# One opening stage in place of two, and a conditioning round moved into the layer norm, in a one-core transformer kernel on Trainium2

## The chip, the cores and the metric

The kernel runs on one core of a Trainium2 chip. The metric is the device time of one execution in microseconds (us); lower is better. All computation is in float32. A weight matrix and its input are each split into a high part that TensorE multiplies in a rounded format (fp32r) and a low remainder, and a product is made of three of the four partial products.

## What is computed

The reference is a chain of transformer blocks. The change touches only the first of them, the convolution block of layer 0, on 512 latent and 256 context tokens of width 1024:

```python
sc = silu(c); scc = silu(c_ctx)
mod_lat = sc @ ada_w[i] + ada_b[i]          # i = 0, 1; six vectors of 1024 each
mod_ctx = scc @ ada_w[i] + ada_b[i]
sh1, sc1, g1, sh2, sc2, g2 = split(mod_lat, 6)      # and the same for ctx
a = rmsnorm(h, norm1_g[i]) * (1 + sc1) + sh1
u = a @ w_pw1 + b_pw1
a, g = split(u, 2)
v = dwconv(a * sigmoid(g), w_dw, 31 taps) + b_dw
v = silu(layernorm(v, ln_g, ln_b))
h = h + g1 * (v @ w_pw2 + b_pw2)
```

The rest (feed-forward blocks, window attention, latent attention, memory attention and a mixture of 16 experts) stands in both kernels as it is.

## The kernel before, in words

Activations lie with the 1024 features on 128 partitions in 8 chunks (KD = 8) and the 768 tokens along the free axis. `X` is the residual, `XNH` and `XNL` the high and low part of the input of the next product. The work is a list of stages. Each stage is a block with a program of its own for every engine, and ends in a barrier of all engines. SP (SyncE) issues every load here, on one DMA queue, in the order of its program.

**Conditioning.** The product of the two conditioning vectors with `ada_w` (2 x 1024 x 6144) is cut into rounds of 8 slices, each slice 1 MB (128 partitions x 4 x 512 numbers). The class `Ada` runs rounds `first` to `end`. Its slices go through a ring of four buffers `ADAW`: `load` (L383) fetches slice n, `multiply_slice` (L405) waits for it and makes four products of 512 columns and counts the semaphore `used`, and SP may load slice n + 4 when slice n is used. After the eighth slice ScalarE copies the result into `ADAR` (`keep_round`, L422), TensorE turns it onto the partitions (`turn_round`, L414), and VectorE adds the bias and makes `MOD`, `GAIN` and `G1B` (`finish`, L431 to L441). Round 0 yields shift and scale of the first norm, rounds 1 and 2 the gate and the other vectors of layer 0, round 3 the shift and scale of layer 1's first norm, which no stage needs before the feed-forward stage of layer 0 is over.

**Stage `start`** loads three small tensors (`PRM`, `IDENT`, `DELTA`) and makes the silu of the conditioning vectors (`SC`).

**Stage `ada`** (`condition`) runs round 0. SP loads its eight slices, then the residual `X` (3 MB), then the first four weight units `RAW` of `pw1` (0.5 MB each). ScalarE and VectorE then split units 0 and 1 into `WHI` (L472) and `WLO` (L480).

**Stage `pw1`** (`gated_convolution`) begins with the class `Norm`: ScalarE squares the 8 chunks of `X` (L546), TensorE sums them over the partitions (L506), ScalarE takes the root (L549), VectorE inverts it (L572), TensorE spreads it over the partitions (L514). Then the 8 chunks pass through VectorE (`SQ`, L579), ScalarE (`SCALED` L556, which needs `MOD` and `GAIN`, and `XNH` L560) and VectorE (`XNL` L582), and `multiply_first` (L329) multiplies units 0 and 1 chunk by chunk as these come. The other 14 units follow (L278). Beside them VectorE convolves chunks 0 to 3 with 31 taps each (L592, L595). Chunks 4 to 7 of the convolution are made on TensorE (`convolve`, L758) at the end of the stage, out of copies of `V` shifted by 8 tokens (`V4`, 16 small copies per chunk, `shift_chunk`, L635). ScalarE moves each result back (`keep_chunk`, L677). Rounds 1, 2 and 3 of the conditioning stand between and behind them on TensorE:

```python
            convolve(0)
            for i in range(ada.rounds):
                convolve(i + 1)
                ada.multiply_round(pe, i)
```

**Stage `pw2`** (`project`) begins with `LayerNormSilu`: TensorE sums for the mean (L506), VectorE centres (L831), ScalarE squares (L798), TensorE sums (L506), ScalarE takes the root into `NARROW` (L802), VectorE inverts it (L834), TensorE spreads it (L514), and the chunks pass VectorE (L841), ScalarE (L808, L811) and VectorE (L845). `multiply_first` takes units 0 and 1, and units 2 to 7 follow. Each unit's result is scaled on ScalarE (L882) and added to `X` on VectorE (L900). The split of unit 2's weights (L249, L260) waits for the end of unit 0.

## Time and profile before

| what | value |
|---|---|
| median of 3 runs | 2690.73 us (2686.09 to 2698.99) |
| profiled execution | 2687.36 us, its span 2685.5 us |
| TensorE (PE) busy | 2437.6 us, 91% of the span |
| VectorE (DVE) busy | 1207.5 us, 45% |
| ScalarE (ACT) busy | 841.2 us, 31% |
| HBM read | 380.22 MB, 142 GB/s over the span |

The profiled execution took 1.9 us more than its span. The busy share is an average over all stages. The change acts only on the first 420 us or so, and there the question is at each place which engine or transfer the others wait for. So the rows below are of the timeline (instructions in order of time, with the idle time before them and what ended it) and of windows (busy time of each engine, granted TensorE clock and DMA share in a stretch).

### The profile page before, as it was taken

What the parts mean: (1) busy time and instruction counts of PE and PEld (TensorE: products, weight loads), DVE (VectorE), ACT (ScalarE), POOL (GpSimd) and SP (SyncE); (2) the same over time, 40 slices, a digit from 0 to 9 for tenths busy, and PEclk for the clock granted to TensorE, in tenths of its full rate; (3) what the DMA queues carried; (4) which work ended last, traced back from release to release, by engine and by line L of the source; (5) the groups of instructions that cost most, each with busy time, mean ns of one, the idle gap of its engine ahead of it and who ended that gap; (6) DMA issues with size and microseconds to landing.
All of it is one profiled execution on the core that took longest, in us unless ns stands there. A gap on an engine that the chain in (4) does not pass through costs nothing. (4 is left out here: it accounts for less than half of the span.)

```text
span 2685.5 us, 34858 instructions
## 1 busy us (share of the span) xinstructions
PE 2437.6 (91%) x14152; PEld 1744.2 (65%) x14152; DVE 1207.5 (45%) x1785; ACT 841.2 (31%) x1290; POOL 29.7 (1%) x57
## 2 busy tenths in 40 slices
PE   4988798999999989899899999987997889999987
PEld 2873376888888876567688888865885653333322
DVE  2598144553255323375465465654543332222223
ACT  3210145332133223276443244355434321000001
POOL 0000000000000000100000000000000000000000
PEclk7998798999999999899899999999999889999998
DMA  5137511121112222400223232210340359999996
GB/s 228 56 89 254 203 48 40 63 72 62 56 62 69 73 102 113 172 1 25 80 100 110 79 105 98 78 53 5 114 133 21 144 198 411 408 411 411 411 414 244
DMA packets 93555, 390.85 MB, mean 146 GB/s; under 512 B 9072, under 2 KB 33904, under 8 KB 65264
## 3 DMA queue, kind: packets, MB, share of 16 engines
q1 hardware_dynamic: 93424, 388.97, 38.9%
q8 instruction: 98, 1.61, 0.2%
q14 instruction: 33, 0.27, 0.0%
HBM read 380.22 MB, written 2.10 MB: 142 GB/s over the span
## 5 line engine op out<-in xcount | busy, mean ns | idle before, releaser
L278 PE MATMUL PS<-XNH,WHI 128*128 128x512 f32 (+1 forms) x1888 | 593.0, 358 | 26.0 <-DVE WLO L260 10.1
L260 DVE TENSOR_TENSOR WLO<-RAW,WHI 128x1024 fp32r<-128x1024 f32 (+3 forms) x226 | 279.2, 1236 | 722.6 <-ACT WHI L249 722.5
L278 PE MATMUL PS<-XNH,WLO 128*128 128x512 f32 (+1 forms) x1888 | 587.9, 355 | 0.0
L278 PE MATMUL PS<-XNL,WHI 128*128 128x512 f32 (+1 forms) x1888 | 587.3, 355 | 0.0
L249 ACT ACTIVATE WHI<-RAW 128x1024 fp32r<-128x1024 f32 (+3 forms) x226 | 241.5, 1068 | 890.5 <-PE PS L278 870.5
L278 PEld LDWEIGHTS PS<-XNH,WHI 128*128 128x128 f32 x1888 | 320.6, 189 | 86.6 <-issue 19.9
L278 PEld LDWEIGHTS PS<-XNL,WHI 128*128 128x128 f32 x1888 | 320.5, 189 | 52.6 <-issue 1.0
L278 PEld LDWEIGHTS PS<-XNH,WLO 128*128 128x128 f32 x1888 | 320.0, 189 | 51.8
L2565 PE MATMUL PS<-RAWM,XS 128*64 128x512 f32 x912 | 216.5, 602 | 19.0 <-DMA RAWM<-experts 18.3
L278 PE MATMUL PS<-HH,WHI 128*128 128x512 f32 (+1 forms) x528 | 158.4, 354 | 0.1
L278 PE MATMUL PS<-HH,WLO 128*128 128x512 f32 (+1 forms) x528 | 158.2, 354 | 0.0
L278 PE MATMUL PS<-HL,WHI 128*128 128x512 f32 (+1 forms) x528 | 158.2, 354 | 0.0
L2565 PEld LDWEIGHTS PS<-RAWM,XS 128*64 128x64 f32 x912 | 59.0, 136 | 143.3 <-issue 76.3
L595 DVE SCALAR_TENSOR_TENSOR C<-V,PRM,C (+1 forms) x120 | 126.0, 1050 | 11.8 <-DVE C L595 9.4
L2699 DVE TENSOR_TENSOR X<-PS,X 128x1024 f32<-128x1024 f32 x64 | 76.8, 1222 | 99.6 <-PE PS L2598 99.6
L2565 PE MATMUL PS<-RAWM,HT 128*64 128x512 f32 x456 | 106.7, 601 | 0.0
L278 PEld LDWEIGHTS PS<-HH,WHI 128*128 128x128 f32 x528 | 86.4, 188 | 15.4 <-DVE HL L1015 0.9
L278 PEld LDWEIGHTS PS<-HH,WLO 128*128 128x128 f32 x528 | 86.4, 188 | 14.6
L278 PEld LDWEIGHTS PS<-HL,WHI 128*128 128x128 f32 x528 | 86.4, 188 | 14.5
L405 PE MATMUL PS<-ADAW,SC 128*32 128x512 f32 x384 | 61.9, 755 | 32.8 <-DMA ADAW<-ada 32.8
L1007 DVE SCALAR_TENSOR_TENSOR Y<-PS,PRM,Y 128x511 f32<-128x511 f32 (+1 forms) x132 | 83.2, 658 | 10.6 <-DVE Y L1002 9.7
L2731 DVE TENSOR_TENSOR HT<-PS,SIL 128x512 f32<-128x512 f32 x16 | 11.1, 692 | 165.5 <-PE PS L2585 165.5
(346 smaller groups left out, 2681.7 us busy)
## 6 DMA issues: line engine op xcount, KB each, us to landing
RAWM<-experts SPq DMA_DIRECT2D x171, 1024.0 KB, 16.2
ADAW<-ada SPq DMA_DIRECT2D x48, 1024.0 KB, 8.3
RAW<-up SPq DMA_DIRECT2D x88, 512.0 KB, 3.2
RAW<-down SPq DMA_DIRECT2D x32, 704.0 KB, 4.1
X<-experts SPq DMA_DIRECT2D x21, 1024.0 KB, 18.4
RAW<-pw SPq DMA_DIRECT2D x24, 512.0 KB, 3.4
V<-V SPq DMA_DIRECT2D x64, 101.0 KB, 2.6
RAW<-qkv SPq DMA_DIRECT2D x12, 512.0 KB, 3.3
```

The source lines that it names most:

```text
L249: act.activation(prog.WHI[:, at % SPLITS, 0:to.length], prog.RAW[:, at % RAWS, 0:to.length], ACT.Copy).then_inc(prog.weights_hi, 1)
L260: dve.tensor_tensor(prog.WLO[:, at % SPLITS, 0:to.length], prog.RAW[:, at % RAWS, 0:to.length], f32(prog.WHI[:, at % SPLITS, 0:to.length]) ...
L278: last = pe.matmul(prog.PS[:, to, a:b], w, x[:, k, a:b], start=(k == 0 and n == 0), stop=(k == g.k - 1 and n == 2))
L405: last = pe.matmul(self.products[n // KD][32 * j:32 * j + 32, :], self.prog.SC[:, k, :], self.ring[:, n % ADA_RING, j * 512:(j + 1) * 512] ...
L595: steps.did(dve.scalar_tensor_tensor(out, v, w, out, ALU.mult, ALU.add))
L1007: ins = dve.scalar_tensor_tensor(Y[:, s, a:b - 1], prog.PS[:, slot, a + 1:b], coef(grp, i, s, 2), Y[:, s, a:b - 1], ALU.mult, ALU.add)
L2565: last = pe.matmul(ps[64 * half:64 * half + 64, :], x(k), moe.half[slot](2 * n + half), start=(k == 0), stop=(k == KD - 1))
L2699: dve.tensor_tensor(x, PAIRS_PS[pair], x, ALU.add).then_inc(added, 1)
L2731: dve.tensor_tensor(HT[:].rearrange("p c h s -> p (c h s)"), BT_PS, SIL[:].rearrange("p c h s -> p (c h s)"), ALU.mult).then_inc(hidden, 1)
```

## The change

The stage `ada` is gone. Its parts stand in `start` and `pw1`:

- In `start`, SP issues, behind the three small loads, the residual in two halves of four chunks, and the first four slices of round 0.
- In `pw1`, SP issues `RAW` units 0 and 1, then slices 4 to 7 as buffers come free, then units 2 and 3.
- TensorE makes the sums of the norm, slices 0 to 3, the spread, slices 4 to 7, and the turn. ScalarE makes squares and root, the split of units 0 and 1, `ADAR`, and only then the chunks. VectorE makes the first two chunks of `SQ`, then `WLO` and `finish`, then the rest.
- In the tail of `pw1`, only rounds 1 and 2 are left. The order is convolve 0, convolve 1, round 1, convolve 2, convolve 3, round 2. The copies for chunk 3 are issued ahead of slice 8 and not of slice 10. Behind the last slice, SP issues the first three slices of round 3 into three buffers of their own (`ADAL`).
- `pw2` is a function of its own, `convolution_output`. Its TensorE multiplies slices 0 and 1 of round 3 ahead of the spread, 2 and 3 behind it, and 4 to 7 behind units 0 and 1, waits until ScalarE has kept the round (their sum lies in the bank that unit 2 writes), and turns it between units 6 and 7. SP loads slice n (3 to 7) when slice n - 3 is used, and all of that ahead of its weight loads.

```diff
+def load_first_slices(prog, sp):
+    prog.first_ring = prog.at("ADAW_0", [P, ADA_RING, 4 * 512], F32, prog.arena + 45536)
+    for n in range(2):
+        sp.dma_start(prog.X[:, 4 * n:4 * n + 4, :], prog.dram["xT"][:, 4 * n:4 * n + 4, :]).then_inc(prog.x_landed[n], 16)
+    for n in range(ADA_RING):
+        sp.dma_start(prog.first_ring[:, n, :], prog.dram["ada"][n]).then_inc(prog.ada_first[n], 16)
...
-def condition(prog, first):
...
+            for u in range(RAWS):
+                if u == SPLITS:
+                    first.load_rest(sp)
+                sp.dma_start(prog.RAW[:, u, 0:g.length], g.src[u]).then_inc(prog.raw_landed[u], 16)
...
             for n in range(ADA_RING, KD * ada.rounds):
-                if n == KD + 2:
+                if n == KD:
                     shift_chunk(3)
                 sp.wait_ge(ada.used, n - ADA_RING + 1)
                 ada.load(sp, n)
+            sp.wait_ge(convolved, 3)
+            for n, slot in enumerate(late_ring):
+                sp.dma_start(slot, prog.dram["ada"][3 * KD + n]).then_inc(prog.ada_landed[n], 16)
...
         def _(act):
-            before.on_scalar(act)
+            before.statistics_on_scalar(act, lambda k: act.wait_ge(prog.x_landed[k // 4], 16))
+            for u in range(SPLITS):
+                act.wait_ge(prog.raw_landed[u], 16)
+                act.activation(prog.WHI[:, u, 0:g.length], prog.RAW[:, u, 0:g.length], ACT.Copy).then_inc(prog.weights_hi, 1)
+            first.keep_round(act, 0)
+            act.wait_ge(first.step, 2)
+            before.chunks_on_scalar(act)
...
-            before.on_tensor(pe)
+            before.sums_on_tensor(pe)
+            for n in range(ADA_RING):
+                first.multiply_slice(pe, n)
+            before.spread_on_tensor(pe)
+            for n in range(ADA_RING, KD):
+                first.multiply_slice(pe, n)
+            first.turn_round(pe, 0)
...
             convolve(0)
-            for i in range(ada.rounds):
-                convolve(i + 1)
-                ada.multiply_round(pe, i)
+            convolve(1)
+            ada.multiply_round(pe, 0)
+            convolve(2)
+            convolve(3)
+            ada.multiply_round(pe, 1)
...
+def convolution_output(prog, g, gate, bias):
...
+        def _(sp):
+            for n in range(3, KD):
+                sp.wait_ge(ada.used, n - 2)
+                ada.load(sp, n)
+            for u in range(g.n):
+                load_ahead(prog, sp, g, u // 4, u % 4)
...
+                ins.then_inc(scaled, 1)
+                if u == 0:
+                    ada.keep_round(act, 0)
...
+            norm.on_tensor(pe)
+            pe.nop().then_inc(psum_free, 4)
+            multiply_first(prog, pe, g, prog.XNH, prog.XNL, lambda u: BOTH, psum_free, chunks_of(pe, norm))
+            for n in range(4, KD):
+                ada.multiply_slice(pe, n)
+            pe.wait_ge(ada.kept, 1)
+            for u in range(2, g.n):
+                multiply(prog, pe, g, u // 4, u % 4, prog.XNH, prog.XNL, BOTH, psum_free)
+                if u == 6:
+                    pe.wait_ge(psum_free, 4 + 5)
+                    ada.turn_round(pe, 0)
```

SP, from the program's start to the first weight loads of `pw1`'s loop (`xT` is the residual in memory, `ada` the conditioning weights, `pw` the weights of `pw1` and `pw2`). Before:

```order
L345 DMA DELTA<-delta 128x32
L173 UNCONDITIONAL_BRANCH
L452 UNCONDITIONAL_BRANCH
L383 DMA ADAW_127<-ada 128x2048 x8
L456 DMA X<-xT 128x6144
L458 DMA RAW<-pw 128x1024 x4
```

Now:

```order
L357 DMA DELTA<-delta 128x32
L344 DMA X<-xT 128x3072 x2
L346 DMA ADAW_101<-ada 128x2048 x4
L175 UNCONDITIONAL_BRANCH
L625 UNCONDITIONAL_BRANCH
L640 DMA RAW<-pw 128x1024 x2
L402 DMA ADAW_101<-ada 128x2048 x4
L640 DMA RAW<-pw 128x1024 x2
```

The residual moved from behind all eight slices to ahead of them, across the first barrier, and two weight units moved ahead of slices 4 to 7.

SP, from the last weight unit of `pw1`'s own loads to the loads of the feed-forward stage (`V` is the shifted copy). Before:

```order
L238 DMA RAW<-pw 128x1024
L383 DMA ADAW_244<-ada 128x2048 x4
L635 DMA V_2_239<-V_235 32x808 x16
L383 DMA ADAW_244<-ada 128x2048 x6
L635 DMA V_2_239<-V_235 32x808 x16
L383 DMA ADAW_244<-ada 128x2048 x14
L173 UNCONDITIONAL_BRANCH
L862 UNCONDITIONAL_BRANCH
L238 DMA RAW<-pw 128x1024 x4
```

Now:

```order
L402 DMA ADAW_146<-ada 128x2048 x4
L634 DMA V_1_141<-V_137 32x808 x16
L402 DMA ADAW_146<-ada 128x2048 x8
L662 DMA ADAL_147<-ada 128x2048
L662 DMA ADAL_148<-ada 128x2048
L662 DMA ADAL_149<-ada 128x2048
L175 UNCONDITIONAL_BRANCH
L899 UNCONDITIONAL_BRANCH
L402 DMA ADAL_147<-ada 128x2048
L402 DMA ADAL_148<-ada 128x2048
L402 DMA ADAL_149<-ada 128x2048
```

Of the 24 slices of the tail 16 are left in it, 3 are issued at its end, and 5 stand in `pw2` ahead of its weight loads.

TensorE in `pw2`, around its spread (L494) and around unit 2 (L280; units 0 and 1 are L331):

```order
L486 MATMUL PS<-TMP_2458,ONES 32x64 x4
L424 MATMUL PS<-ADAL_147,SC 32x512 x4
L424 MATMUL PS<-ADAL_148,SC 32x512 x4
L494 MATMUL PS<-NARROW_2460,IDENT 128x128 x4
L494 MATMUL PS<-NARROW_2460,IDENT 128x64 x4
L424 MATMUL PS<-ADAL_149,SC 32x512 x4
L424 MATMUL PS<-ADAL_147,SC 32x512 x4
L331 MATMUL PS<-XNH,WHI 128x512
...
L331 MATMUL PS<-XNH,WLO 128x256
L424 MATMUL PS<-ADAL_148,SC 32x512 x4
L424 MATMUL PS<-ADAL_149,SC 32x512 x4
L424 MATMUL PS<-ADAL_147,SC 32x512 x4
L424 MATMUL PS<-ADAL_148,SC 32x512 x4
L280 MATMUL PS<-XNH,WHI 128x512
```

None of the L424 rows stood here before. There the spread followed the sums, and unit 2 followed units 0 and 1.

## Rows read from the trace of the kernel before

**Rows 1.** Windows: the opening, and a stretch of pw1's tail (columns in the first line).
```profile
core 0: us, PE busy (x) PEld busy (x) DVE busy (x) ACT busy (x) POOL busy (x), PEclk, DMA share, GB/s
0.00:40.00 40.00, 15.11 (x72) 3.31 (x72) 3.24 (x7) 4.58 (x6) 0.20 (x4) 0.75 0.88 356
...
240.00:260.00 20.00, 15.00 (x112) 4.48 (x116) 19.33 (x20) 0.60 (x1) 0.00 (x0) 0.74 1.01 354
```
**Rows 2.** Timeline of the opening: start, duration, engine, line, operation, idle before.
```profile
4.50 0.22 ACT L351 ACTIVATE SC<-PRM 128x16 f32<-128x16 f32 x1 [1.85 <-DMA DELTA<-delta]
4.98 14.58 SPq L383 DMA_DIRECT2D ADAW<-ada  x8
...
9.83 1.94 PE L405 MATMUL PS<-ADAW,SC 128*32 128x512 f32 x8 [9.83 <-DMA ADAW<-ada]
...
27.18 1.94 PE L405 MATMUL PS<-ADAW,SC 128*32 128x512 f32 x8 [1.43 <-DMA ADAW<-ada]
...
31.97 0.18 DVE L437 SCALAR_TENSOR_TENSOR GAIN<-MOD,PRM 128x16 f32<-128x16 f32 x1
35.74 1.06 ACT L472 ACTIVATE WHI<-RAW 128x1024 fp32r<-128x1024 f32 x1 [5.96 <-DMA RAW<-pw]
...
39.63 1.58 ACT L546 ACTIVATE SQ<-X 128x768 f32<-128x768 f32 x2 [1.56 <-PEq L173]
...
53.28 1.30 ACT L556 ACTIVATE SCALED<-SQ,MOD,GAIN 128x512 f32<-128x512 f32 x2 [5.03 <-DVE SQ L579]
...
56.60 0.98 PE L329 MATMUL PS<-XNH,WHI 128*128 128x512 f32 x2 [4.34 <-DVE XNL L582]
```
**Rows 3.** Timeline of TensorE in pw1's tail.
```profile
236.09 3.61 PE L405 MATMUL PS<-ADAW,SC 128*32 128x512 f32 x32
242.48 1.93 PE L405 MATMUL PS<-ADAW,SC 128*32 128x512 f32 x8 [2.78 <-DMA ADAW<-ada]
...
252.98 11.88 PE L758 MATMUL PS<-V,DIAG 128*32 128x512 f32 x128
264.69 1.89 PE L405 MATMUL PS<-ADAW,SC 128*32 128x512 f32 x16
...
284.92 10.54 PE L758 MATMUL PS<-V,DIAG 128*32 128x512 f32 x128
295.27 3.62 PE L405 MATMUL PS<-ADAW,SC 128*32 128x512 f32 x32
```
**Rows 4.** Timeline: ScalarE and VectorE at the end of pw1.
```profile
310.86 0.60 ACT L422 ACTIVATE ADAR<-PS 128x512 f32<-128x512 f32 x1 [14.29 <-PE PS L405]
...
312.61 0.32 DVE L431 TENSOR_TENSOR MOD<-PS,PRM 128x64 f32<-128x64 f32 x2 [41.82 <-PE PS L414]
```
**Rows 5.** Timeline of SP's queue in pw1's tail (start, length of issuing).
```profile
237.35 9.92 SPq L383 DMA_DIRECT2D ADAW<-ada  x6
247.38 11.94 SPq L635 DMA_DIRECT2D V<-V  x16
```
**Rows 6.** Timeline of pw2: the inversion, the spread, units 0 and 1, unit 2.
```profile
331.54 1.35 DVE L834 RECIPROCAL NARROW<-NARROW 128x192 f32<-128x192 f32 x1 [3.14 <-ACT NARROW L802]
332.95 3.67 PE L514 MATMUL PS<-NARROW,IDENT 128*128 128x128 f32 x16 [2.41 <-DVE NARROW L834]
...
340.75 0.98 PE L329 MATMUL PS<-XNH,WHI 128*128 128x512 f32 x2 [4.13 <-DVE XNL L845]
...
361.05 0.62 PE L278 MATMUL PS<-XNH,WHI 128*128 128x512 f32 x2 [1.41 <-DVE WLO L260]
```
**Rows 7.** Windows on the granted clock (PEclk) after waits: pw1's tail, pw2, pw1's start.
```profile
299.00:309.00 10.00, 4.94 (x24) 0.56 (x24) 0.00 (x0) 0.00 (x0) 0.00 (x0) 0.73 0.93 378
...
340.70:345.00 4.30, 4.25 (x15) 3.66 (x16) 4.12 (x8) 4.07 (x5) 0.00 (x0) 0.56 0.00 0
345.00:359.60 14.60, 14.60 (x84) 12.45 (x82) 7.80 (x13) 8.49 (x10) 0.00 (x0) 1.00 0.00 1
...
56.60:61.00 4.40, 4.40 (x14) 3.72 (x14) 3.90 (x5) 4.30 (x8) 0.00 (x0) 0.50 0.02 4
```

More of the change, by code:

```diff
@@ L362, with ring_of, __init__ @@
 ADA_ROUNDS = 2 * ADA_SLICES // 4
+def ring_of(tile):
+    return [tile[:, s, :] for s in range(ADA_RING)]
 class Ada:
-    def __init__(self, prog, first, end, ring, rows, products=None, turned_at=None, sem=None):
+    def __init__(self, prog, first, end, ring, rows, products=None, turned_at=None, sem=None, landed=None):
         self.prog, self.first, self.rounds = prog, first, end - first
-        self.ring, self.rows = ring, rows
+        self.slots, self.rows = ring, rows
+        self.n_slots = len(ring)
         self.products = [prog.PS[:, 0, 0:512]] * self.rounds if products is None else products
@@ L376, in __init__ @@
         sem = sem or prog.sem
-        self.landed = [sem(f"ada_landed{s}") for s in range(ADA_RING)]
+        self.landed = [sem(f"ada_landed{s}") for s in range(self.n_slots)] if landed is None else landed
         self.used, self.kept, self.turned = sem("ada_used"), sem("ada_kept"), sem("ada_turned")
@@ L381, in load @@
     def load(self, sp, n):
-        sp.dma_start(self.ring[:, n % ADA_RING, :], self.src[KD * self.first + n]).then_inc(self.landed[n % ADA_RING], 16)
+        sp.dma_start(self.slots[n % self.n_slots], self.src[KD * self.first + n]).then_inc(self.landed[n % self.n_slots], 16)
     def load_first(self, sp):
-        for n in range(ADA_RING):
+        for n in range(self.n_slots):
             self.load(sp, n)
     def load_rest(self, sp):
-        for n in range(ADA_RING, KD * self.rounds):
-            sp.wait_ge(self.used, n - ADA_RING + 1)
+        for n in range(self.n_slots, KD * self.rounds):
+            sp.wait_ge(self.used, n - self.n_slots + 1)
             self.load(sp, n)
```

122 lines of the change are left out of this document (75 added, 47 removed).

## The prediction

> **What bounds the kernel now.** I read the windows first, to see which resource is full in the stretches that the change touches, and then the timeline of each place. In the opening 40 us the DMA queues are full (share 0.88, 356 GB/s) while TensorE is busy for 15.11 us [rows 1]. In the tail of `pw1` the same holds: DMA share 1.01 between 240 and 260 us with TensorE waiting for slices [rows 1, 3]. So both places wait for bytes or for a chain behind them, and an engine's busy share tells little.
>
> The opening is three chains in series [rows 2]. The slices come from 9.83 us on, and the eighth at 27.18, so one takes (27.18 - 9.83) / 7 = 2.48 us, or 423 GB/s. `GAIN` is ready at 31.97 + 0.18 = 32.15. Then come `X` and the weights (35.74) and a barrier, and only at 39.63 do the squares begin. Statistics last until ScalarE's first scaled chunk at 53.28, and the first product stands at 56.60. The statistics need only `X`. `GAIN` is first needed at 53.28, 21 us after it is ready.
>
> The tail is a chain of TensorE and slices. VectorE ends its taps 41.82 us before `MOD` [rows 4], so it doesn't bound the end. A round takes TensorE 3.61 us for four slices that lie in the ring, and then follows DMA: the last one goes from 295.27 to 310.86, 15.59 us [rows 3, 4].
>
> **The opening.** The small loads have landed at 4.50 [rows 2]. Now `X` and the first slices are issued behind them with no barrier between, so bytes flow on from about 4.5. Ahead of the last slice's landing stand `X` (3.15 MB), eight slices (8.39 MB) and two units (1.05 MB), 12.58 MB, at 423 GB/s 29.7 us: it lands at 34.2, against 27.18 before. Can SP keep the queue full? `X` has landed at about 12. The last four squares take 4 x 0.79 = 3.2 us, so sums end near 16, and slices 0 to 3 at the lower clock take 1.94 each [rows 2]: the last is used near 24. Slices 4 to 7 are therefore issued between 18 and 24, while the queue holds work until 24.2 (12 for `X`, four slices to 21.9, two units to 24.4). It just suffices. Root, inversion and spread, which took 53.28 - 39.63 = 13.7 us with the squares before, now end near 28, under the remaining slices. The split of the two units hides there too. From the last slice to `GAIN` it was 32.15 - 27.18 = 4.97 us, so `GAIN` is at 39.2, and from ScalarE's first scaling to the first product it was 56.60 - 53.28 = 3.32: first product at 42.5. That is **-14.1 us**. Lower bound of the gain: if slice 0 is used late and the last four slices come as slowly as they come when SP waits for one buffer each, two to three more intervals of 2.48 are lost, gain 7. Upper bound: 15.
>
> After that `pw1` has the same work in the same order and shifts as a whole.
>
> **The tail of `pw1`.** I keep the old times here. Up to 252.98 nothing changes: convolve 0 and 1 and one round. Convolve 2 runs to 264.69 [rows 3]. Now convolve 3 follows at once; it took 295.27 - 284.92 = 10.35 us in one place and 11.71 in the other, which began at the lower clock. I take 10.35, since it now stands right behind a dense stretch: 275.0. Then the last round, whose first four slices must lie in the ring. SP issues the copies right behind slice 7 (near 240) for 11.9 us [rows 5], then slices 8 to 11, which land from about 257 to 269 even if the copies hold the queue for as long as they are issued; cover 6 us. So the round lasts 15.59 as before and `ADAR` is kept at 290.6 and not at 310.86: **-20.2 us**. If convolve 3 takes 11.71, -18.9. If the cover fails altogether (four slices still to come at 275), +10 on that, -10. The three late slices are issued behind all others and land by 298, over 10 us ahead of their first use.
>
> **The norm of `pw2`.** Slices 0 and 1 stand in TensorE's wait ahead of 332.95, which is 2.41 us long [rows 6]. At 1.94 each they last 3.9, at the rate of 3.61 for four 1.8. So the spread is late by at most 1.5 us. But the spread took 3.67 there at the lower clock, and denser work ahead of it may shorten it. Slice 3 is issued when slice 0 is used (about 332) and lands about 5 us later (issued at 237.35, multiplied at 242.48 [rows 3, 5]), 337.5; slices 2 and 3 end by 339.5, ahead of the first chunk at 340.75. TensorE then comes to units 0 and 1 from work and not from a wait of 4.13 us. These ran from 340.75 to 359.65 (361.05 - 1.41), 18.9 us, with the granted clock at 0.56 in the first 4.3 us (most of it the lower level, 1.2 GHz) and at 1.00 behind [rows 7]. With the full clock from the start, 0.44 x 4.3 = 1.9 less. I take **-1.9**, between +1.5 (all slices slow, no clock won) and -3.5.
>
> **Slices 4 to 7 of `pw2`.** This is the new wait. Slices 4, 5 and 6 lie in the three buffers, but slice 7 takes slice 4's buffer and is issued only when that is used. The pattern is that of a round: from its first slice to the fifth's arrival 242.48 - 236.09 = 6.39 us [rows 3]. So slice 7 starts at 359.65 + 6.4 = 366.0. Then 0.9 to 1.9 for it (over a round's slices that come by DMA the granted clock is 0.73 [rows 7], so either is possible), and 0.7 for ScalarE's copy (310.86 + 0.60, and a semaphore): unit 2 begins at 367.7 to 368.6 and not at 361.05, +6.7 to +7.6. Behind unit 2's start ScalarE has been waiting too, with the split of unit 3 behind it, and SP with the weight loads; both are needed a whole unit later, so they cost nothing. TensorE has waited some 3.7 us and more. After waits of 4.13 and 4.34 us it had 0.56 and 0.50 of the clock for the next 4.3 [rows 2, 6, 7], which costs half of that, +1.9. I take **+9.0**, between +6.5 and +10.
>
> The Trainium skill, TensorE: Matmul & The Clock Gate, section The HAM clock gate, says that the throttled state is the default, that activity releases it, and that work arriving in bursts behind DMA waits pays the lower clock again each time. By that, the gain of a warm start and the loss behind the new wait both stand (-1.9 and +1.9), and the change is no free filling of waits. Those two sizes are taken from the rows, and the trace agrees.
>
> **The turn** between units 6 and 7 stands in a dense stretch: from `ADAR`'s copy at 310.86 to `MOD` at 312.61 it is 1.75, less the copy's 0.60 [rows 4], **+1.2**.
>
> For slice 7 the row gives about 5.1 us from issue to use. The Trainium skill, DMA: Bandwidth & Descriptors, section Anatomy of one DMA, gives a fixed cost of about 2.0 us and a peak of 436 GB/s. An estimate from these, 2.0 + 1.05 MB / 436 GB/s = 4.4, would make the wait 0.7 shorter and the sum -26.7; I go by the row.
>
> **Sum:** -14.1 - 20.2 - 1.9 + 9.0 + 1.2 = **-26.0 us**. The profiled execution, 2687.36, becomes 2661.4. The median of the runs shown is 3.4 above it and theirs spread over 13 us, so I state the median: 2690.73 - 26.0 = **2664.7**. The rest of the program comes behind one barrier and shifts.
>
> **The rivals.**
>
> 1. *One of the two places gives half.* Either SP finds the ring full in the opening (gain 7), or the copies delay slices 8 to 11 (gain 10). For it: in the opening the queue and the use of the buffers meet within about 1 us. Against: the tail has a cover of 6 us. Sum -16 to -19, a time of 2672 to 2675. Chance 0.12.
> 2. *`pw2` eats most.* Round 3 is fetched there one buffer at a time. If each of slices 3, 4 and 7 has TensorE waiting a full 5.1 us, with the clock lost behind each (1.9), two more such waits cost 14. Sum -12, a time of 2679. For it: the ring is of three and not four. Against: slices 4 to 6 have the 19 us of units 0 and 1 to land. Chance 0.07.
> 3. *Slower than before, by the clock.* `pw1`'s 16 units now start out of a thin stretch of slices. If the clock stayed at its lower level there, each unit would take 8.5 us more (a unit is 18.9 - 1.9 = 17.0 for two). It turns the result slower from four such units on (34 against 26); at six it is 2716. Against: the clock came back within 4.4 us of the first product in the same place, after an equally thin opening [rows 7]. Chance 0.03.
> 4. *More than forecast*, where the tail's convolve and the norm take the better ends and slice 7 comes early: -31, 2660. This lies inside my forecast's own spread.
>
> **How the numbers follow.** My forecast holds 0.78. The likeliest case's terms give -20 to -33 (2658 to 2671), and a median of few runs moves by some 4 us. Taking in rival 1 the range is 2653 to 2676, which leaves out rivals 2 and 3 and a little on the low side. What a measurement can tell from no change is 0.5%, 13.5 us: faster means below 2677.3. All of the forecast and of rival 1 lie below, and a part of rival 2 by the noise: faster 0.90, same 0.07, slower 0.03.
>
> **What would show it.** The first L331 product at 42.5 us, 14 us sooner, with slices arriving without a gap; the last `ADAR` of `pw1` some 34 us sooner than 310.86, with copies and slices 8 to 11 landed before convolve 3 ends; no idle time ahead of the first chunk of `pw2` longer than 2 us and a PEclk near 1.00 in its first 4 us; between unit 1 and unit 2 about 8 us, with one DMA wait in it of some 3.7 us ahead of the fourth slice, and a lower clock behind. I am wrong if VectorE or the queue ends one of these waits instead, if the slices' spacing in the opening grows beyond 2.5 us, or if unit 2 doesn't wait.

## The result, and the profile after

| | before | changed |
|---|---|---|
| median, 8 runs each | 2698.76 us | 2664.97 us |
| lowest and highest | 2686.09, 2704.20 | 2661.64, 2680.35 |
| span of the profiled execution | 2685.5 us | 2663.0 us |

The ratio of changed to before is 0.990, with a 95% interval of 0.9883 to 0.9918: some 27 us less, between 22 and 32. Forecast were 26.0 us less and 2664.7 us. The two medians lie 33.8 us apart, which is more than the interval allows: runs of one kernel spread over 18 to 19 us, and the medians alone are less steady than the ratio over all runs. That the median fell within 0.3 us of the forecast is luck. The forecast was counted down from 2690.73, the median of three runs, and the median of eight is 8 us higher.

A table of marks shows where the time went. Each mark is the start of a row of the timeline, for the profiled execution of either kernel. A second profiled execution of the changed kernel (run `e10_changed_again` below) stands beside it.

| mark | before | changed | change of the stretch, changed against before | changed again |
|---|---|---|---|---|
| first product of `pw1` | 56.60 | 44.66 | -11.9 | 43.45 |
| first product of convolve 0 | 212.71 | 200.51 | -0.3 | 199.12 |
| last `ADAR` of `pw1` | 310.86 | 280.21 | -18.5 | 279.97 |
| first product of `pw2` | 340.75 | 308.29 | -1.8 | 308.08 |
| unit 2 of `pw2` | 361.05 | 335.49 | +6.9 | 333.67 |
| first square of the feed-forward stage | 415.77 | 393.07 | +2.9 | 390.80 |
| end of the span | 2685.5 | 2663.0 | +0.2 | 2672.5 |

**The opening.** Timeline of the changed kernel (start, duration, engine, line, operation, idle before), to be held against [rows 2]:

```profile
2.14 0.91 SPq L344 DMA_DIRECT2D X<-xT  x2
3.09 2.51 SPq L346 DMA_DIRECT2D ADAW<-ada  x4
...
9.83 1.58 ACT L531 ACTIVATE SQ<-X 128x768 f32<-128x768 f32 x2 [4.36 <-DMA X<-xT]
...
19.03 6.28 SPq L402 DMA_DIRECT2D ADAW<-ada  x4
...
26.89 1.82 DVE L572 TENSOR_TENSOR SQ<-X,PS 128x768 f32<-128x768 f32 x2 [6.53 <-PE PS L494]
...
28.89 1.06 PE L424 MATMUL PS<-ADAW,SC 128*32 128x512 f32 x8 [2.03 <-DMA ADAW<-ada]
...
36.35 1.94 PE L424 MATMUL PS<-ADAW,SC 128*32 128x512 f32 x8 [0.55 <-DMA ADAW<-ada]
...
41.35 1.30 ACT L543 ACTIVATE SCALED<-SQ,MOD,GAIN 128x512 f32<-128x512 f32 x2 [2.40 <-DVE GAIN L456]
...
44.66 0.98 PE L331 MATMUL PS<-XNH,WHI 128*128 128x512 f32 x2 [3.79 <-DVE XNL L577]
```

The statistics are over at 26.89, under the slices, and what ScalarE's first scaling waits for is now `GAIN`. The four last slices arrive 2.48 us apart (28.89 to 36.35), so the queue never ran empty. The last one came 2.1 us later than I had put it (34.2).

**The tail.** TensorE's timeline, to be held against [rows 3]:

```profile
223.79 3.60 PE L424 MATMUL PS<-ADAW,SC 128*32 128x512 f32 x32
229.95 1.94 PE L424 MATMUL PS<-ADAW,SC 128*32 128x512 f32 x8 [2.56 <-DMA ADAW<-ada]
232.43 1.94 PE L424 MATMUL PS<-ADAW,SC 128*32 128x512 f32 x8 [0.55 <-DMA ADAW<-ada]
234.92 1.84 PE L424 MATMUL PS<-ADAW,SC 128*32 128x512 f32 x8 [0.55 <-DMA ADAW<-ada]
239.40 1.47 PE L424 MATMUL PS<-ADAW,SC 128*32 128x512 f32 x8 [2.65 <-DMA ADAW<-ada]
241.57 1.87 PE L433 MATMUL PS<-PRM,ADAR 128*128 128x8 f32 x8 [0.70 <-ACT ADAR L441]
243.37 22.51 PE L787 MATMUL PS<-V,DIAG 128*32 128x512 f32 x256
265.71 3.60 PE L424 MATMUL PS<-ADAW,SC 128*32 128x512 f32 x32
```

Convolve 2 and 3 follow each other (22.3 us for both), and the next round begins with four slices in the ring. But in the first round slice 7 is late: it comes 4.48 us behind slice 6, not 2.48. The last `ADAR` of `pw1` stands 30.7 us sooner than before (280.21 against 310.86), where I had said some 34.

**The stage `pw2`.** Timeline around the norm, to be held against [rows 6]:

```profile
299.31 2.92 PE L424 MATMUL PS<-ADAL,SC 128*32 128x512 f32 x16
...
302.16 2.00 PE L494 MATMUL PS<-NARROW,IDENT 128*128 128x128 f32 x16
304.09 1.07 PE L424 MATMUL PS<-ADAL,SC 128*32 128x512 f32 x8
...
306.11 1.06 PE L424 MATMUL PS<-ADAL,SC 128*32 128x512 f32 x8 [0.95 <-DMA ADAL<-ada]
...
308.29 0.98 PE L331 MATMUL PS<-XNH,WHI 128*128 128x512 f32 x2 [1.11 <-DVE XNL L884]
```

Slices 0 and 1 fill the wait ahead of the spread, and the spread takes 2.00 us and not 3.67. Around unit 2:

```profile
326.91 2.78 PE L424 MATMUL PS<-ADAL,SC 128*32 128x512 f32 x24
...
332.83 1.94 PE L424 MATMUL PS<-ADAL,SC 128*32 128x512 f32 x8 [3.14 <-DMA ADAL<-ada]
334.83 0.60 ACT L441 ACTIVATE ADAR<-PS 128x512 f32<-128x512 f32 x1 [6.63 <-PE PS L424]
...
335.49 1.01 PE L280 MATMUL PS<-XNH,WHI 128*128 128x512 f32 x2 [0.72 <-ACT ADAR L441]
```

Slices 4 to 6 are multiplied at once, slice 7 is waited for, and unit 2 starts 335.49 - 326.91 = 8.58 us behind unit 1's end, where it had been 1.41. The windows tell the clock (columns as in [rows 1]):

```profile
303.00:308.00 5.00, 3.22 (x27) 1.34 (x26) 2.76 (x5) 2.72 (x3) 0.00 (x0) 1.00 0.96 401
308.30:312.00 3.70, 3.70 (x13) 3.17 (x14) 3.52 (x7) 3.48 (x5) 0.00 (x0) 0.55 0.93 359
...
335.50:340.00 4.50, 4.50 (x17) 3.87 (x18) 2.09 (x2) 2.00 (x3) 0.00 (x0) 0.62 0.35 133
```

Behind the new wait the granted clock is 0.62 for 4.5 us, and at the first product of `pw2` it fell to 0.55 although it had been 1.00 under slices 2 and 3.

### The profile page after: what moved, and what is told of

It reads as the page before. It is cut to its first block and busy times, and to the rows that moved or that the text cites. A ratio compares the mean times of both kernels' runs of the same rounds, so it can differ in the third digit from the quotient of the medians.

```text
span 2663.0 us, 34851 instructions
## 1 busy us (share of the span) xinstructions
PE 2430.8 (91%) x14152; PEld 1742.9 (65%) x14152; DVE 1207.0 (45%) x1785; ACT 841.0 (32%) x1290; POOL 29.7 (1%) x57
## 5 line engine op out<-in xcount | busy, mean ns | idle before, releaser
L280 PE MATMUL PS<-XNH,WHI 128*128 128x512 f32 (+1 forms) x1888 | 593.8, 359 | 25.3 <-DVE WLO L262 8.9
L280 PE MATMUL PS<-XNL,WHI 128*128 128x512 f32 (+1 forms) x1888 | 587.0, 355 | 0.0
L280 PE MATMUL PS<-XNH,WLO 128*128 128x512 f32 (+1 forms) x1888 | 586.4, 355 | 0.0
L280 PEld LDWEIGHTS PS<-XNH,WHI 128*128 128x128 f32 x1888 | 320.6, 189 | 86.8 <-issue 19.5
L280 PEld LDWEIGHTS PS<-XNL,WHI 128*128 128x128 f32 x1888 | 321.2, 190 | 53.0 <-issue 1.0
L280 PEld LDWEIGHTS PS<-XNH,WLO 128*128 128x128 f32 x1888 | 319.8, 189 | 52.3
L280 PE MATMUL PS<-HH,WHI 128*128 128x512 f32 (+1 forms) x528 | 158.3, 354 | 0.0
L280 PE MATMUL PS<-HL,WHI 128*128 128x512 f32 (+1 forms) x528 | 158.1, 353 | 0.0
L280 PE MATMUL PS<-HH,WLO 128*128 128x512 f32 (+1 forms) x528 | 158.0, 353 | 0.0
L590 DVE SCALAR_TENSOR_TENSOR C<-V,PRM,C (+1 forms) x120 | 125.9, 1050 | 11.8 <-DVE C L590 9.4
L2797 DVE TENSOR_TENSOR X<-PS,X 128x1024 f32<-128x1024 f32 x64 | 76.8, 1221 | 100.6 <-PE PS L2696 100.6
L280 PEld LDWEIGHTS PS<-HH,WHI 128*128 128x128 f32 x528 | 86.4, 188 | 15.4 <-DVE HL L1113 0.9
L280 PEld LDWEIGHTS PS<-HL,WHI 128*128 128x128 f32 x528 | 86.4, 188 | 14.5
L280 PEld LDWEIGHTS PS<-HH,WLO 128*128 128x128 f32 x528 | 86.4, 188 | 14.4
L1105 DVE SCALAR_TENSOR_TENSOR Y<-PS,PRM,Y 128x511 f32<-128x511 f32 (+1 forms) x132 | 83.2, 658 | 10.6 <-DVE Y L1100 9.7
L1100 DVE SCALAR_TENSOR_TENSOR Y<-PS,PRM,Y 128x511 f32<-128x511 f32 (+1 forms) x132 | 82.6, 653 | 0.0
```

The costliest lines, as they stand in the source:

```text
L280: last = pe.matmul(prog.PS[:, to, a:b], w, x[:, k, a:b], start=(k == 0 and n == 0), stop=(k == g.k - 1 and n == 2))
L590: steps.did(dve.scalar_tensor_tensor(out, v, w, out, ALU.mult, ALU.add))
L1100: ins = dve.scalar_tensor_tensor(Y[:, s, a + 1:b], prog.PS[:, slot, a:b - 1], coef(grp, i, s, 0), Y[:, s, a + 1:b], ALU.mult, ALU.add)
L1105: ins = dve.scalar_tensor_tensor(Y[:, s, a:b - 1], prog.PS[:, slot, a + 1:b], coef(grp, i, s, 2), Y[:, s, a:b - 1], ALU.mult, ALU.add)
L2797: dve.tensor_tensor(x, PAIRS_PS[pair], x, ALU.add).then_inc(added, 1)
```

## The experiments

Each run is read at the marks above. Totals of single executions of one kernel differ by 10 us and more, and the last section shows where a large part of that arises. So a few microseconds are told from stretches, not from totals. The changed kernel was profiled twice: the "first" execution is that of the result above, the "second" that of `e10_changed_again`.

| run | median us (runs) | ratio to before, 95% interval |
|---|---|---|
| `e1_opening_only` | 2683.86 (10) | 0.9945, 0.9923 to 0.9968 |
| `e2_no_round3` | 2665.34 (4) | 0.9897, 0.9863 to 0.9931 |
| `e3_slices_inside` | 2669.65 (4) | 0.9908, 0.9875 to 0.9941 |
| `e4_copies_late` | 2665.31 (4) | 0.9897, 0.9860 to 0.9933 |
| `e5_units_behind_slices` | 2673.99 (2) | 0.9912, 0.9890 to 0.9935 |
| `e6_dense_norm` | 2666.21 (1) | |
| `e7_small_loads_behind` | 2673.92 (1) | |
| `e8_combined` | 2662.99 (4) | 0.9878, 0.9847 to 0.9909 |
| `e9_tail_only` | 2688.45 (6) | 0.9975, 0.9952 to 0.9997 |
| `e10_changed_again` | 2671.35 (6) | 0.9913, 0.9890 to 0.9937 |
| `e11_combined_again` | 2667.40 (6) | 0.9889, 0.9862 to 0.9916 |

### The two places apart

`e1_opening_only` has the new opening and before's tail and `pw2`:

```diff
-        ada = Ada(prog, 1, 3, ring_of(ring), rows)
+        ada = Ada(prog, 1, 4, ring_of(ring), rows)
...
-            convolve(0)
-            convolve(1)
-            ada.multiply_round(pe, 0)
-            convolve(2)
-            convolve(3)
-            ada.multiply_round(pe, 1)
+            convolve(0)
+            for i in range(ada.rounds):
+                convolve(i + 1)
+                ada.multiply_round(pe, i)
...
-    add("pw2", lambda: convolution_output(prog, gemms["pw2"], ...
+    add("pw2", lambda: project(prog, gemms["pw2"], ...
```

> The new opening with the tail of pw1 and the stage pw2 of the kernel before. Theory (the opening, the tail and pw2 add up independently): the first product of pw1 stands near 44.7 us as in the changed kernel (56.6 before), everything behind it is as before, so the span is 12 us shorter than before's, about 2673.5. Rival (a later part gives the opening's gain back, or the tail's gain needs the new opening): the span is under 8 us or over 16 us shorter, and the stretch from the first product to the last ADAR of pw1 is not the 254.3 us of before.

`e9_tail_only` is its complement, with before's stage `ada` and the new tail and `pw2`:

```diff
-            load_first_slices(prog, sp)
...
-            before.sums_on_tensor(pe)
-            for n in range(ADA_RING):
-                first.multiply_slice(pe, n)
-            before.spread_on_tensor(pe)
-            for n in range(ADA_RING, KD):
-                first.multiply_slice(pe, n)
-            first.turn_round(pe, 0)
+            before.on_tensor(pe)
...
+    add("ada", lambda: condition(prog, order[0]))
```

> The tail of pw1 and the stage pw2 of the changed kernel, with the opening of the kernel before (stage ada and all). Theory (the parts add): the first product stands at 56.6 us as before, the stretch from the convolution's first product to the last ADAR of pw1 is some 18.5 us shorter than before's 98.1, pw2 from there to the first square of the feed-forward stage is 8 us longer than before's 104.9, and that square comes 10.5 us sooner than 415.8, near 405. Rival (with the old opening the tail's gain is another, or the opening's 12 us weren't all its own): that square is under 6 or over 15 us sooner.

First product of `pw1` (first line) and first square of the feed-forward stage (second), timeline of `e1_opening_only`:

```profile
42.95 0.98 PE L331 MATMUL PS<-XNH,WHI 128*128 128x512 f32 x2 [3.79 <-DVE XNL L577]
...
404.30 6.74 ACT L531 ACTIVATE SQ<-X 128x768 f32<-128x768 f32 x8 [1.30 <-PEq L175]
```

The same of `e9_tail_only`:

```profile
56.62 0.98 PE L331 MATMUL PS<-XNH,WHI 128*128 128x512 f32 x2 [4.35 <-DVE XNL L615]
...
403.90 1.58 ACT L569 ACTIVATE SQ<-X 128x768 f32<-128x768 f32 x2 [1.62 <-PEq L175]
```

At the square, before stood at 415.77. The opening alone is 11.5 us ahead of that and the tail with `pw2` alone 11.9, together 23.3, where the changed kernel is 22.7 ahead in its first execution and 25.0 in its second. So the parts add, to within the 2.3 us between those two, and neither needs the other. Of the 13.65 us that `e1_opening_only` is ahead at its first product, 11.5 are left at the square; 1.6 of the loss lies between the last `ADAR` and the first product of `pw2` (31.5 us against 29.9 before), and half of that is the turn there, at the lower clock (1.88 us against 1.06). The stretch from the first product to the last `ADAR` was 254.7 us in `e1_opening_only` (254.3 before). In `e9_tail_only` the tail took 80.2 us (98.15 before), and from the last `ADAR` to the square it was 111.5 (104.9 before). The gain of the opening at its first product was 13.65 us in `e1_opening_only` and 11.9 and 13.15 in the two executions of the changed kernel. About half of this spread is the turn behind the last slice, which took 1.88 us at the lower clock in the first execution and 1.06 at the full one in the two others. The rest is the last slice itself, which took 1.94, 1.58 and 1.52 us, and its arrival (36.35, 36.30 and 35.86).

### What round 3 costs in its new place

`e2_no_round3` leaves the round out of `pw2`, with constants for what it would yield:

```diff
-            for n in range(4, KD):
-                ada.multiply_slice(pe, n)
-            pe.wait_ge(ada.kept, 1)
...
-                    step = ada.finish(dve, [(1, 0, 2)], [(1, 0)])
+                    dve.memset(prog.MOD[1][:, 0:16, :], 0.5)
+                    dve.memset(prog.GAIN[1][0][:], 1.0)
```

> The changed kernel with round 3 of the conditioning left out of pw2: its five late loads, eight slices, copy, turn and bias are gone, and layer 1's first norm gets constants for its shift and scale. It prices what round 3 costs in its new place. Theory: it costs the wait between units 1 and 2 (8.6 us against 1.4), half a clock behind it (1.6) and the turn (1.1), and it gives back 1.7 on the spread, which runs at the full clock only because slices stand ahead of it; so the span is 8 us shorter than the changed kernel's (about 2655) and the spread takes 3.7 us again in place of 2.0. Rival (the spread's gain has nothing to do with the slices): the spread stays at 2.0 us and the span is 10 us shorter.

Timeline of `e2_no_round3`, the spread, the first product and the first square:

```profile
304.12 3.67 PE L494 MATMUL PS<-NARROW,IDENT 128*128 128x128 f32 x16 [2.41 <-DVE NARROW L868]
...
311.93 0.98 PE L331 MATMUL PS<-XNH,WHI 128*128 128x512 f32 x2 [4.13 <-DVE XNL L879]
...
386.96 1.58 ACT L531 ACTIVATE SQ<-X 128x768 f32<-128x768 f32 x2 [1.35 <-PEq L175]
```

The spread is back at 3.67 us, so its 1.7 us are a gift of the slices ahead of it, as the theory had it. It took 3.68 in `e1_opening_only` too, and 2.00 in all ten executions that have the slices there. From the first product to the square it is 75.03 us here, 75.02 before, and 84.78 and 82.72 in the two executions of the changed kernel: the round costs 7.7 to 9.8 us there. It gives back 2.9 ahead of the first product (30.98 against 28.08). Net that is 4.8 to 6.9 us, where I had expected 8. But 0.8 of the 2.9 is the clock at `pw1`'s last turn, which both kernels have (1.88 us here, 1.06 there) and which no edit set. Without it the round costs 5.6 to 7.7. Out of `pw1` it took a whole round, for which the tail is 17.3 to 18.5 us shorter.

### What the wait between units 1 and 2 is

`e3_slices_inside` gives the loads the time of units 0 and 1:

```diff
-            multiply_first(prog, pe, g, prog.XNH, prog.XNL, lambda u: BOTH, psum_free, chunks_of(pe, norm))
-            for n in range(4, KD):
-                ada.multiply_slice(pe, n)
+            inside = {3: 4, 5: 5, 6: 6}
+            multiply_first(prog, pe, g, prog.XNH, prog.XNL, lambda u: BOTH, psum_free, chunks_of(pe, norm),
+                           between=lambda k: k in inside and ada.multiply_slice(pe, inside[k]))
+            ada.multiply_slice(pe, 7)
```

> The changed kernel with slices 4, 5 and 6 of round 3 multiplied inside units 0 and 1 (behind chunks 3, 5 and 6) and only slice 7 behind them. Nothing is left out. Theory (the wait between units 1 and 2 is the latency of slice 7, whose load waits for slice 4's buffer): slice 7 has landed, units 0 and 1 get 2.7 us longer, unit 2 begins about 1.7 us behind them and not 8.6 behind, at the full clock: 4.2 + 1.6 = about 6 us shorter than the changed kernel, span near 2657. Rival (the wait is the chain through ScalarE, which copies the round only behind unit 0's scaling): the wait stays over 4 us and the gain is under 2 us.

Timeline of `e3_slices_inside`, from the first product to unit 2:

```profile
310.97 0.58 PE L331 MATMUL PS<-XNH,WHI 128*128 128x512 f32 x2 [1.08 <-DVE XNL L886]
...
331.52 1.07 PE L426 MATMUL PS<-ADAL,SC 128*32 128x512 f32 x8
...
333.35 0.62 PE L280 MATMUL PS<-XNH,WHI 128*128 128x512 f32 x2 [0.76 <-ACT ADAR L443]
```

Slice 7 is there, and unit 2 begins 1.83 us behind units 0 and 1, at the full clock (0.62 us for the pair and not 1.01). From the first product to unit 2 it is 22.4 us and not 27.2, and from there to the square 56.2 and not 57.6: 6.2 us less. The rival, a chain through ScalarE, is out, since ScalarE's program was not touched. That 6.2 meets the 6 expected is partly luck, because here the first products of `pw2` ran at the full clock and in the first execution of the changed kernel at the lower one, which this edit doesn't set. Against the second execution (82.72 us from the first product to the square), in which they ran at the full clock too, the 78.60 are 4.1 less. The other executions at the full clock with slices 4 to 7 behind units 0 and 1 and nothing added to the norm took 82.2 to 83.2 (`e5`, `e7`, `e9`), the two others with the slices inside 78.8 and 78.7 (`e8`, `e11`). So the edit is worth about 4 us, and 4.2 of wait and 1.6 of clock had been expected.

### Why slice 7 was late in the tail

```diff
-                if n == KD:
+                if n == KD + 2:
                     shift_chunk(3)
```

> The changed kernel with the copies for chunk 3 issued ahead of slice 10, as before, and not ahead of slice 8. Theory (the copies move at half the bytes per second and share the queue with slices 5 to 7 that were issued just ahead of them): slice 7 of the tail's first round arrives 2.5 us behind slice 6 and not 4.5, so the step from round to convolve 2 is 16.9 us and not 19.6, and the copies still land before convolve 3: 2 to 2.7 us shorter than the changed kernel. Rival (the 2.7 us are chance of that execution or the clock): slice 7 is late again, or convolve 3 now waits for its copies, and the span doesn't change or grows.

Timeline of `e4_copies_late`, slices 4 and 7 of the tail's first round and the turn:

```profile
229.07 1.90 PE L424 MATMUL PS<-ADAW,SC 128*32 128x512 f32 x8 [2.38 <-DMA ADAW<-ada]
...
236.54 1.94 PE L424 MATMUL PS<-ADAW,SC 128*32 128x512 f32 x8 [1.43 <-DMA ADAW<-ada]
239.19 1.88 PE L433 MATMUL PS<-PRM,ADAR 128*128 128x8 f32 x8 [0.71 <-ACT ADAR L441]
```

From slice 4 to slice 7 it is 7.47 us, against 9.45 in the changed kernel, 9.12 and 9.20 in `e2_no_round3` and `e3_slices_inside`, which have the same order of copies. All thirteen executions part in the same way: 9.0 to 9.5 us in the eight with the early copies, 7.45 to 7.51 in the five with the late ones (before, `e1`, `e4`, `e8`, `e11`). So slice 7's lateness hangs on that order, though slice 7 is issued ahead of the copies either way. The step from the round to convolve 2 took 17.9 us and not 19.6 (16.9 was expected: the turn fell into the lower clock), and convolve 3 did not wait for its copies. The whole tail took 79.2 us against 79.7 to 81.3 in the eight with the early copies and an otherwise equal tail. In the two other tails of this kind with late copies, `e8_combined` and `e11_combined_again`, it took 77.3 and 76.8. There the turn and convolve 2 ran at the full clock, and convolve 3 began 1.3 and 1.7 us behind the end of convolve 2, as the rival had feared. The queue still moved the bytes at the copies' rate until about then (232 GB/s from 248 to 249 us in `e8_combined`, 380 in the next microsecond), so the copies are the likely cause of this gap. That is not shown, since the profile names nothing that ended it.

### What the opening is bound by

`e5_units_behind_slices` moves one megabyte from ahead of the last slice to behind it:

```diff
+            first.load_rest(sp)
             for u in range(RAWS):
-                if u == SPLITS:
-                    first.load_rest(sp)
                 sp.dma_start(prog.RAW[:, u, 0:g.length], g.src[u]).then_inc(prog.raw_landed[u], 16)
...
+            first.keep_round(act, 0)
             for u in range(SPLITS):
                 act.wait_ge(prog.raw_landed[u], 16)
...
-            first.keep_round(act, 0)
...
-                first.finish(dve, [(0, 0, 2)], [(0, 0)])
+                    if u == 0:
+                        first.finish(dve, [(0, 0, 2)], [(0, 0)])
```

> The changed kernel with weight units 0 and 1 of pw1 loaded behind slices 4 to 7 of round 0 and not ahead of them; ScalarE copies the round first and splits the units then, VectorE puts the bias between the two remainders. Theory (the opening is bound by the bytes ahead of the last slice): the last slice arrives two half-megabyte loads sooner, 33.9 and not 36.35 us; the units land at about 35.1 and 36.4, their splits end near 40, and the first product stands near 42.2 to 43 and not 44.7: 1.5 to 2.5 us sooner. Rival (the split is now the last thing, or SP can't issue the last slices sooner because TensorE uses the first ones late): the last slice arrives no more than 1 us sooner, or the first product is where it was or later, because it waits for WLO.

Timeline of `e5_units_behind_slices`, the last slice, the first scaling and the first product:

```profile
33.74 1.93 PE L424 MATMUL PS<-ADAW,SC 128*32 128x512 f32 x8 [1.44 <-DMA ADAW<-ada]
...
38.89 1.31 ACT L543 ACTIVATE SCALED<-SQ,MOD,GAIN 128x512 f32<-128x512 f32 x2 [0.66 <-DVE GAIN L456]
...
42.21 0.98 PE L331 MATMUL PS<-XNH,WHI 128*128 128x512 f32 x2 [3.94 <-DVE XNL L577]
```

The last slice comes 2.6 us sooner for 1.05 MB less ahead of it (2.5 us at 423 GB/s), and the first product 2.45 us sooner. The opening is bound by bytes ahead of the last slice. Without this edit the last slice came at 35.86 to 36.84 us in eight executions, so the 2.6 are clear of their scatter.

`e7_small_loads_behind` asks about the 2.1 us that I had missed:

```diff
-            sp.dma_start(prog.IDENT[:], prog.dram["ident"]).then_inc(loaded, 16)
-            sp.dma_start(prog.DELTA[:], prog.dram["delta"]).then_inc(loaded, 16)
             load_first_slices(prog, sp)
+            sp.dma_start(prog.IDENT[:], prog.dram["ident"]).then_inc(prog.small_landed, 16)
+            sp.dma_start(prog.DELTA[:], prog.dram["delta"]).then_inc(prog.small_landed, 16)
...
-            act.wait_ge(loaded, 48)
+            act.wait_ge(loaded, 16)
...
```

> The changed kernel with the two small loads IDENT and DELTA issued behind the residual and the first four slices, with waits of their own. I had put the last slice of round 0 at 34.2 us, and it came at 36.35. Theory (the two small loads, with rows of 512 and 128 bytes, slow the queues down while the residual starts): the first half of the residual lands at least 1 us sooner than 9.83 us and the last slice with it. Rival (the 2.1 us are the time from a transfer's last byte to its landing together with the queues' start, which order doesn't change): both stay within 0.5 us.

Timeline of `e7_small_loads_behind`, the first squares and the last slice:

```profile
8.41 1.58 ACT L532 ACTIVATE SQ<-X 128x768 f32<-128x768 f32 x2 [4.03 <-DMA X<-xT]
...
36.15 1.78 PE L425 MATMUL PS<-ADAW,SC 128*32 128x512 f32 x8 [0.56 <-DMA ADAW<-ada]
```

Half of each theory: the residual's first half lands 1.4 us sooner, the last slice 0.2. Of the 1.4 us, 0.9 is that SP issues the residual at 1.20 and not at 2.14. The 0.2 is within the scatter of the last slice, so it is no gain, and why the last slice doesn't follow the residual no run shows. With 12.58 MB at 423 GB/s ahead of it, a last slice at 36.35 means a stream that counts from 6.6 us, and I had let it count from 4.5, when the small loads had landed. Windows of the first execution allow an estimate of how these 2.1 us part. Up to 34.8 us the queues had moved 13.3 MB (383 GB/s from the start), about what the small loads (0.6 MB) and the 12.58 MB make, and the product that needs the last of it began some 1.5 us later. The rest, some 0.6, lies at the start: from 4 to 6 us they moved 272 GB/s, from 8 us on 421. What fills the 1.5 us between the last bytes and the product stays open.

### Whether the short waits in the norm cost the clock

```diff
         for n in range(2, 4):
             self.ada.multiply_slice(pe, n)
+            for j in range(4):
+                pe.matmul(self.prog.PS[32 * j:32 * j + 32, 2, 512:1024], self.prog.SC[:, 0, :], self.prog.X[:, j, 0:512], start=True, stop=True)
```

> The changed kernel with eight extra products of 512 columns in pw2's norm, four behind slice 2 and four behind slice 3 of round 3, written to a bank that nothing reads; nothing is left out. It asks why units 0 and 1 of pw2 still started at the lower clock behind slices 2 and 3. Theory (the clock falls because of the waits of about 1 us ahead of slice 3 and ahead of the first product): with them filled the first product runs at the full clock, units 0 and 1 take 17.0 to 17.5 us to the start of slice 4 and not 18.6. Rival (the clock at the first product follows what TensorE did well before, in the norm's thin sums, and not these two waits): the first products take 0.98 and 0.84 us again and units 0 and 1 take 18.6.

Timeline of `e6_dense_norm`, the first product of `pw2`:

```profile
310.98 0.59 PE L331 MATMUL PS<-XNH,WHI 128*128 128x512 f32 x2 [0.47 <-DVE XNL L886]
```

The full clock from the start, and 17.1 us for units 0 and 1. By itself this one run would bear the theory out, but `e10_changed_again` does not let it:

> The changed kernel again, beside the combined one and the tail alone. Theory: ratio to before 0.989 to 0.992, some 23 to 27 us less. It is also one more look at whether the first products of pw2 stand at the lower clock (0.98 and 0.84 us a piece) or the full one (0.59 and 0.5): if the waits of about 1 us ahead of them decide it, they are slow again as in the first look; if it is a matter of where the execution stands, either can come.

Timeline of `e10_changed_again`, in which the program is the changed kernel's own:

```profile
299.32 2.34 PE L424 MATMUL PS<-ADAL,SC 128*32 128x512 f32 x16
...
308.08 0.59 PE L331 MATMUL PS<-XNH,WHI 128*128 128x512 f32 x2 [1.39 <-DVE XNL L884]
```

It waits 1.39 us ahead of its first product, longer than the 1.11 of the first execution, and starts at the full clock. The windows show it:

```profile
303.00:308.00 5.00, 3.01 (x25) 1.12 (x24) 2.97 (x6) 2.90 (x4) 0.00 (x0) 1.00 1.01 419
308.10:312.00 3.90, 3.90 (x22) 3.39 (x23) 3.72 (x7) 3.68 (x5) 0.00 (x0) 1.00 1.00 414
```

Nine executions have the slices in the norm and nothing added to its waits. Seven of them start at the full clock, `e7_small_loads_behind` even behind a wait of 2.10 us, and two (the first of the changed kernel and `e4_copies_late`) at the lower. So these waits alone don't decide it. In the two that start at the lower clock slices 0 and 1 had taken 2.92 and 2.82 us, in the others 1.90 to 2.41. What does decide stays open.

### The three edits together

`e8_combined` takes the edits of `e3_slices_inside`, `e4_copies_late` and `e5_units_behind_slices` together.

> The changed kernel with three edits together: slices 4 to 6 of round 3 inside units 0 and 1 of pw2, the copies for chunk 3 ahead of slice 10 in pw1's tail, and weight units 0 and 1 behind slices 4 to 7 in the opening. Theory (the three terms add): -6 -1.7 -2 = about -9.5 us at the first square of the feed-forward stage (393.1 in the changed kernel), so 383.5, and a median some 10 us below the changed kernel's. Rival (one of them gives back at another place): over 387 there.

> The combined kernel again, in the same rounds as the changed one. Theory: the first square of the feed-forward stage 8 to 10 us sooner than in the changed kernel beside it, and in the medians a difference of the same size, if five rounds can show it (ratio to before 0.985 to 0.989). Rival (the gain is one execution's): under 4 us there.

Timeline of `e8_combined`, the first square of the feed-forward stage:

```profile
384.12 1.58 ACT L533 ACTIVATE SQ<-X 128x768 f32<-128x768 f32 x2 [1.62 <-PEq L175]
```

And of `e11_combined_again`:

```profile
382.07 1.58 ACT L533 ACTIVATE SQ<-X 128x768 f32<-128x768 f32 x2 [1.62 <-PEq L175]
```

These are 9.0 us less than 393.07 (9.5 expected) and 8.7 less than the 390.80 of `e10_changed_again`, which was measured beside it. Taken crosswise the difference is 6.7 to 11.0. The medians beside each other are 2667.40 and 2671.35, and the intervals of the two ratios overlap, so the whole time doesn't settle it. At the marks both executions agree: the square stands 31.7 and 33.7 us ahead of before's, in place of 22.7 and 25.0. Two terms are still lost here: the gap ahead of convolve 3 that is told above, and in `e11_combined_again` about 1 us in the opening, where the turn ended near 36.4 and `MOD` began only at 37.40, behind VectorE's first `WLO` (36.26 to 37.49).

## Why the prediction was right, point by point

The forecast was 26.0 us less. The ratio over 8 runs each gives 27, between 22 and 32; a later set of 6 against 11 runs (`e10_changed_again`) gives 23, between 17 and 30. At the feed-forward stage the two profiled executions are 22.7 and 25.0 us ahead, at the span's end 22.5 and 13.0, where the last section says what came in between. So the mechanisms held, their sum was some 1 to 3 us too high at the marks, and the whole time can't tell so small a difference.

- **The opening**, forecast -14.1, measured -11.9 and -13.2. The mechanism was right: statistics under the slices, no gap in the stream, `GAIN` last. Two terms after it held in the first execution: 4.96 us from the last slice to `GAIN` (4.97 before), and 3.3 from the first scaling to the first product. In the second the first of them was 3.8, because the last slice and the turn ran partly or wholly at the full clock. The mis-sized term is the landing of the last slice, 34.2 forecast and 36.35 measured, because I let the stream count from the landing of the small loads at full rate and gave the last bytes no time to reach the product.
- **The tail**, forecast -20.2, measured -18.5, -17.3 and (alone) -17.9. Convolve 2 and 3 took 22.34 us (22.06 forecast), and the last round 14.5 (15.6). The step that failed is "up to 252.98 nothing changes". I asked whether the early copies leave slices 8 to 11 in time, which they did, and not what they do to slice 7, already issued but not landed: 2.0 us. The turn behind it ran at the lower clock for all of its 1.87 us, where it had taken 1.33 before; that is not the copies' doing, for in `e4_copies_late` it took 1.88. `e4_copies_late` shows the 2.0 us, and the other four executions with late copies agree. Together convolve 2 began 2.6 us late, of which the shorter last round gave 1.1 back in the first execution and 0.1 in the second.
- **The norm with units 0 and 1**, forecast -1.9, measured -2.1, but made otherwise: 1.7 on the spread and 0.3 on units 0 and 1 (18.6 us). In the second execution it was 1.7 and 1.8. The bound of -3.5 was the better value for that one. The prediction had a full clock in units 0 and 1 as its reason and named the shorter spread only as a possibility, so the total of the first execution came right by luck.
- **Slices 4 to 7**, forecast 6.7 to 7.6 of wait and 1.9 of clock, measured 7.2 of wait, and 2.9 for clock and turn together (3.1 forecast). Slice 7 was issued at 328.04 and multiplied at 332.83, 4.8 us; the row I took gave 5.1. An estimate from the Trainium skill's figures (DMA: Bandwidth & Descriptors, section Anatomy of one DMA) gives 4.4, and the measurement decides: it is 0.4 us more. The page fits those figures to loads that GpSimd issues, and here SP issues them, which the prediction had not said.
- **The rule on bursts.** The 0.62 of the clock behind the new wait is near the 0.56 and 0.50 that the rows behind waits of 4.13 and 4.34 us had shown. The Trainium skill's rule (TensorE: Matmul & The Clock Gate, section The HAM clock gate), that bursts behind DMA waits pay the lower clock again, agrees with unit 2 in all seven executions in which slice 7 is waited for (1.01 us for its first pair). In the three in which it isn't, the first pair takes 0.62. It doesn't settle the first products of `pw2`, which came at either clock behind waits of the same size.
- **The rivals.** The opening did not run short of issues: slices 4 to 7 were issued from 19.03 on and arrived without a gap. `pw2` had one wait of 3.1 us and one of 0.95 for slices, not three of 5. `pw1`'s body kept its length, 155.85 us against 156.11, so the clock did not stay down there. The rows that I named against this rival show 0.50 of the clock for the first 4.4 us and nothing behind them; the trace of the kernel before has 0.98 in the next 5 us (61 to 66), so the argument stands on that.

## What to carry to other kernels

Where a stage waits for a stream of loads, order everything by what is needed last: the work that needs none of the stream goes under it, and bytes that aren't needed before its end go behind it (2.45 us for one megabyte here). Work that is put into a wait brings its own waits along: ask for each of its loads which buffer it takes and when that comes free, and begin the work early enough that the last load has a dense stretch to land in, which was worth about 4 us here, of the 5.6 to 7.7 that the moved round still cost. And ask of a transfer that is issued sooner not only whom it overtakes, but who is still in flight ahead of it.

## What the runs showed of the hardware that I had not expected

**One program, two rates at full clock.** The second execution of the changed kernel is 2.3 us ahead of the first at 391 us and 9.5 us behind it at the end. Both run the same products. Windows of `e10_changed_again`:

```profile
650.00:700.00 50.00, 50.00 (x285) 43.41 (x284) 10.10 (x13) 4.88 (x4) 0.00 (x0) 1.00 0.16 53
```

The same stretch in the first execution:

```profile
650.00:700.00 50.00, 50.00 (x290) 43.75 (x289) 9.92 (x12) 5.91 (x6) 0.00 (x0) 1.00 0.14 48
```

TensorE is never idle in either and the granted clock is 1.00 in both, but 285 instructions were made in 50 us in the one and 290 in the other, 1.7% apart. From the first product with `HH` to the first of `KT` with `QT`, all of it work that no edit touches, it is 517.6 us in one and 509.9 in the other. The thirteen executions fall into two groups: 508.9 to 512.1 in eight (before and the first of the changed kernel among them) and 516.0 to 518.7 in five (`e1`, `e5`, `e7`, `e9`, `e10`). This is 7.7 of the 11.8 us by which the two executions of the changed kernel part behind 391 us, and it is why the experiments are read at marks. Where it comes from no run here shows.

**Copies inside the core hold up a load that is ahead of them.** In the changed kernel the queue's rate fell from about 430 to about 210 GB/s when the 16 copies of 32 partitions came, and the megabyte issued just ahead of them landed 2.0 us late. Windows of the changed kernel, ahead of the copies and in them:

```profile
232.00:234.00 2.00, 1.57 (x8) 0.20 (x8) 1.93 (x3) 0.00 (x0) 0.00 (x0) 0.50 1.02 434
...
238.00:240.00 2.00, 0.60 (x8) 0.16 (x8) 1.96 (x2) 0.00 (x0) 0.00 (x0) 0.98 1.00 205
```

The Trainium skill (DMA: Bandwidth & Descriptors, section Queues, rings and completion order) says that completion is not in the order in which one engine issues. That would allow it, but on which of the 16 DMA engines the copies got ahead, no row here shows.
